# Other strips stream and other beats are set in the first layer, and TensorE adds more rows in the second

## What is computed

```python
def peer_ffn(h, w_q, sub_keys, u, v):          # per block of 128 tokens
    q = (xb @ w_q).reshape(BLK, PEER_HEADS, PEER_QDIM)               # 8 heads x 128
    s1 = einsum('thd,hkd->thk', q[..., :64], sub_keys[:, 0])         # 128 keys each
    s2 = einsum('thd,hkd->thk', q[..., 64:], sub_keys[:, 1])
    v1, i1 = top_k(s1, 16); v2, i2 = top_k(s2, 16)
    sc, ci = top_k(v1[..., :, None] + v2[..., None, :], 16)          # of 256 sums
    e = take(i1, ci // 16) * 128 + take(i2, ci % 16)                 # 16 experts per head
    g = softmax(sc)
    a = gelu(einsum('thkd,td->thk', u[e], xb)) * g
    return einsum('thk,thkd->td', a, v[e])
```

## Time and profile before

| | us |
|---|---|
| median of 3 runs | 2897.95 (2896.8 to 2899.27) |
| the profiled execution, its own time | 2902.58 |
| its span, first to last instruction | 2900.4 |

### The profile page before, as it was taken

The page is one execution under the profiler, slowest core; times in us unless marked ns, Lnnn a source line. Parts: engine busy times, 40 slices in busy tenths (PEclk is TensorE's granted clock), DMA queues, the critical chain, the costliest instruction groups (busy, mean ns, idle before and its releaser), DMA issues.

```text
span 2900.4 us, 27200 instructions
## 1 busy us (share of the span) xinstructions
PE 2284.9 (79%) x7394; PEld 1213.3 (42%) x7394; DVE 2184.6 (75%) x5166; ACT 1183.7 (41%) x3457; POOL 1244.1 (43%) x1049
## 2 busy tenths in 40 slices
PE   9779787788877887786887878877788878886567
PEld 8536442454424554243443434443354434432122
DVE  2688678876878757796688876988679876887664
ACT  3154334344343443445344453435534453433333
POOL 0254335443444333444434543354434444345655
PEclk9899999899999898998899988989889998988989
DMA  6599999999999999999999999999999999999998
GB/s 271 209 418 421 398 398 416 421 421 403 415 420 421 420 375 420 420 418 421 421 393 406 422 421 420 389 416 421 421 402 406 421 421 421 399 421 421 422 422 350
DMA packets 170817, 1170.27 MB, mean 403 GB/s; under 512 B 19668, under 2 KB 19928, under 8 KB 36136
## 3 DMA queue, kind: packets, MB, share of 16 engines
q0 software_dynamic: 147456, 1073.81, 89.7%
q1 hardware_dynamic: 23208, 94.74, 8.3%
HBM read 1164.28 MB, written 4.19 MB: 403 GB/s over the span
## 4 chain that ended last, share of the span: by engine, by line
DMA 28%; DVE 14%; PE 11%; issue 6%; POOL 3%; ACT 3%; POOLq 0%; DVEq 0%; ACTq 0%
DMA ring<-in_uv,pick 26%; PE acc L1723 6%; DVE ring L1094 4%; POOL ring L666 3%; PE ps L1514 3%; DVE side L1085 1%; DMA xc<-h 1%; DMA stream<-in_strips 1%; ACT diag L1368 1%; DVE arena L969 1%; DVE arena L950 1%; DVE arena L1040 1%; DVE arena L1044 1%; DVE arena L951 1%; DVE arena L1031 1%
## 5 line engine op out<-in xcount | busy, mean ns | idle before, releaser
L666 POOL DMA_INDIRECT ring<-in_uv,pick x1024 | 1239.7, 1211 | 1630.5 <-PE acc L1723 1092.9
L1723 PE MATMUL acc<-ring,diag 128*128 128x512 f32 x2988 | 1542.5, 659 | 465.3 <-ACT diag L1368 462.3
L1094 DVE CUSTOM_DVE_ANT_0 ring<-ring,h_now 128x1024 f32<-128x1024 f32 x1024 | 1235.4, 1222 | 490.2 <-DMA ring<-in_uv,pick 474.0
L1723 PEld LDWEIGHTS acc<-ring,diag 128*128 128x128 f32 x2988 | 582.6, 207 | 1287.7 <-ACT diag L1368 702.8
L1357 ACT ACTIVATE gelu<-dots 128x1 f32<-128x1 f32 x1024 | 206.1, 201 | 1264.6 <-DVE dots L1094 1258.0
L1085 DVE SCALAR_TENSOR_TENSOR side<-ring,coef,side 128x1024 f32<-128x1024 f32 x270 | 346.0, 1281 | 23.1 <-ACT coef L1360 23.0
L1360 ACT ACTIVATE coef<-gate,gelu 128x1 f32<-128x1 f32 x1024 | 302.0, 295 | 33.2
L1368 ACT ACTIVATE diag<-ident,coef 128x128 f32<-128x128 f32 x747 | 300.1, 402 | 29.8 <-PE acc L1723 5.5
L1514 PE MATMUL ps<-resident,actT 128*128 128x256 f32 x896 | 220.3, 403 | 14.5 <-ACT actT L1169 14.5
L1514 PEld LDWEIGHTS ps<-resident,actT 128*128 128x128 f32 x896 | 178.1, 202 | 58.9 <-issue 18.2
L1481 PE MATMUL ps<-actT,stream 128*128 128x128 f32 x960 | 124.9, 291 | 23.6 <-DMA stream<-in_strips 22.7
(11 more groups left out here) (198 smaller groups left out, 1454.6 us busy)
## 6 DMA issues: line engine op xcount, KB each, us to landing
stream<-in_strips SPq DMA_DIRECT2D x102, 512.0 KB
resident<-in_strips SPq DMA_DIRECT2D x18, 1024.0 KB, 12.9
ring<-in_uv,pick POOLq DMA_INDIRECT x1024
ring<-in_strips SPq DMA_DIRECT2D x9, 1024.0 KB, 19.6
arena<-in_keys SPq DMA_DIRECT2D x8, 512.0 KB
xc<-in_x SPq DMA_DIRECT2D x4, 512.0 KB
h<-arena SPq DMA_DIRECT2D x4, 512.0 KB, 11.4
xc<-h SPq DMA_DIRECT2D x4, 512.0 KB
```

Of the source, the lines that this page charges most:

```text
L666: pool.indirect_dma_start(ring[:, n % SLOTS, :], None, tables[layer], bass.IndirectOffsetOnAxis(ap=pick[:, col:col + 1], axis=0),).then_in ...
L1094: dve.tensor_tensor_reduce(ring[:, slot, 0:D], ring[:, slot, 0:D], h_now[:], 1.0, 0.0, ALU.mult, ALU.add, dots[:, slot:slot + 1]).then_inc ...
L1723: m = pe.matmul(acc[:, b * 512:(b + 1) * 512], diag[:, turn % 4, :], ring[:, slot, D + b * 512:D + (b + 1) * 512], start=(r == 0 and i == ...
```

## The change

In the first layer the resident strips are 5, 7, 9, 11, 13 and 15 to 18 (v1, v3, r1, r3, out1, out3, pq0 to pq2); 0 to 4, 6, 8, 10, 12, 14 and 19 pass. The beats of stages 1 and 2 are set anew, mostly earlier and further apart; those of stage 0 and of the second layer stay. `VECTOR` changes for "gla" (34 rows per stage instead of 37, none or one in rounds 0 to 2) and for "swa" (none from round 7 on: 19 instead of 34). SP loads the opening's strips in order of number, the keys of the first layer after all its passing strips, the first five resident strips of the second layer after "r" and "y" instead of "v", and in the second layer the bias, the other four resident strips, gain and keys after the first passing strip. POOL's wait for pq1 goes.

```diff
-STREAMED = tuple(s - RESIDENT for s in STRIPS)
+KEPT = ((5, 7, 9, 11, 13, 15, 16, 17, 18), (0, 1, 2, 3, 4, 5, 6, 7, 8))
+PASSING = tuple(tuple(n for n in range(STRIPS[layer]) if n not in KEPT[layer]) for layer in range(2))
+STREAMED = tuple(len(p) for p in PASSING)
...
-SAYS = ({11: "r", 15: "y", 16: "pq0", 17: "pq1", 18: "pq2", 19: "pq3"},
-        {8: "y", 9: "pq0", 10: "pq1", 11: "pq2", 12: "pq3"})
-DONE = [[SAYS[layer].get(n) for n in range(RESIDENT, STRIPS[layer])] for layer in range(2)]
+SAYS = ({1: "q", 3: "k", 19: "pq3"}, {9: "pq0", 10: "pq1", 11: "pq2", 12: "pq3"})
+DONE = [[SAYS[layer].get(n) for n in PASSING[layer]] for layer in range(2)]
...
-GAIN_AT = (13 - RESIDENT, 10 - RESIDENT)
+GAIN_AT = (PASSING[0].index(14), PASSING[1].index(10))
...
     "gla": (
-        ((1, 4, 7),) * 3 + ((0, 2, 4, 6),) + ((1, 4, 7),) * 2 + ((0, 2, 4, 6),) + ((1, 3, 5, 7),) +
-        ((0, 3, 6),) + ((2, 6),) + ((1, 4),) + ((2, 6),) + ((4,),) + ((),) * 3),
+        ((1,),) + ((),) + ((4,),) + ((0, 2, 4, 6),) + ((1, 3, 5, 7),) * 2 + ((0, 2, 4, 6),) + ((1, 3, 5, 7),) +
+        ((0, 2, 4, 6),) + ((1, 3, 5, 7),) + ((1, 4, 7),) + ((4,),) + ((),) * 4),
     "swa": (
-        ((1, 4, 7),) * 2 + ((0, 2, 4, 6),) + ((0, 4),) + ((1, 5),) + ((0, 3, 6),) + ((2, 6),) +
-        ((1, 4, 7),) * 2 + ((2, 6),) + ((1, 3, 5, 7),) + ((0, 3, 6),) + ((),) * 4),
+        ((1, 4, 7),) * 2 + ((0, 2, 4, 6),) + ((0, 4),) + ((1, 5),) + ((0, 3, 6),) + ((2, 6),) + ((),) * 9),
...
     "gla": {
-        "pe": {"hT": 7, "q0": 12, "q1": 24, "k0": 29, "k1": 38, "v0": 43, "v1": 45, "v2": 49, "v3": 52, "attn": 56,
-               "r0": 56, "r1": 56, "r2": 60, "upd": 62, "r3": 62, "o0": 64, "o1": 64, "oT": 69, "out0": 71,
-               "out1": 73, "out2": 76, "out3": 79, "h2T": 84, "pq0": 84, "sc0": 86, "pq1": 88, "sc1": 90, "pq2": 94,
-               "sc2": 94, "pq3": 105, "sc3": 118},
...
+        "pe": {"hT": 7, "q0": 11, "q1": 15, "k0": 18, "k1": 22, "v0": 26, "v1": 28, "v2": 31, "v3": 33, "attn": 38,
+               "r0": 40, "r1": 43, "r2": 46, "upd": 49, "r3": 50, "o0": 54, "o1": 55, "oT": 61, "out0": 64,
+               "out1": 68, "out2": 72, "out3": 76, "h2T": 82, "pq0": 83, "sc0": 86, "pq1": 88, "sc1": 91, "pq2": 94,
+               "sc2": 97, "pq3": 104, "sc3": 112},
...
             def load_kept_ahead(prep):
 
-                said_by(sp, "pe", before(prep), "v")
+                said_by(sp, "pe", before(prep), "r")
                 for n in range(AHEAD):
 
+                    if n == 4:
+                        said_by(sp, "pe", before(prep), "y")
                     released(sp, pick_number(BLOCKS - 2, AHEAD_AT + n - 1, 0))
...
                 for n in range(STREAMED[prep.layer]):
-                    if n == GAIN_AT[prep.layer]:
+                    if n == GAIN_AT[prep.layer] + opening:
+
+                        if prep.layer == 1:
+                            if prep.first:
+                                load_kept_rest(prep)
+
+                            said_by(sp, "pe", prep, "o3")
+                            sp.dma_start(bias_out, b_out).then_inc(bias_loaded, 16)
 
                         said_by(sp, "pe", prep, "oT")
...
+                if prep.layer == 0:
+                    load_keys(prep)
...
-                    elif SAYS[0].get(RESIDENT + n, "r") not in ("r", "y", "pq0"):
-
-                        said_by(pool, "pe", Prep("gla", 0), SAYS[0][RESIDENT + n])
-                        alone(pool, passed["pool"])
...
             def left(prep, n, bank, side):
...
                 for c in range(2):
                     for k in range(KT):
+                        if c == 0 and k % CUT == 0:
+                            cut_loaded(prep, n, k // CUT)
                         i = pe.matmul(ps[:, bank, (2 * side + c) * P:(2 * side + c + 1) * P],
                                       w[:, k, c * P:(c + 1) * P], actT[:, k, :], start=(k == 0),
                                       stop=(k == KT - 1))
+                        if c == 1 and k % CUT == CUT - 1:
+                            cut_done(prep, n, k // CUT, i)
                 return i
```

More of the change, by code:

```diff
@@ L416, in in_ring, with passing @@
         def in_ring(prep, n):
-            return prep.first and prep.layer == 0 and RESIDENT <= n < RESIDENT + SLOTS
+            return prep.first and prep.layer == 0 and n in PASSING[0][:SLOTS]
+        def passing(prep, n):
+            return n in PASSING[prep.layer]
         def weight(prep, n):
-            if n < RESIDENT:
-                return resident[:, n]
+            if not passing(prep, n):
+                return resident[:, KEPT[prep.layer].index(n)]
             if in_ring(prep, n):
-                return ring[:, n - RESIDENT, :].rearrange("p (k c) -> p k c", k=KT)
+                return ring[:, PASSING[0].index(n), :].rearrange("p (k c) -> p k c", k=KT)
             return stream
@@ L511, in load_kept @@
             def load_kept(prep, n):
-                sp.dma_start(resident[:, n].rearrange("p k c -> p (k c)"), strips[prep.layer][n])\
+                sp.dma_start(resident[:, n].rearrange("p k c -> p (k c)"),
+                             strips[prep.layer][KEPT[prep.layer][n]])\
                   .then_inc(res_loaded[n], 16)
             def load_kept_ahead(prep):
-                said_by(sp, "pe", before(prep), "v")
+                said_by(sp, "pe", before(prep), "r")
                 for n in range(AHEAD):
+                    if n == 4:
+                        said_by(sp, "pe", before(prep), "y")
                     released(sp, pick_number(BLOCKS - 2, AHEAD_AT + n - 1, 0))
@@ L528, in load_kept_rest, with load_keys @@
                     load_kept(prep, n)
+            def load_keys(prep):
+                said_by(sp, "pe", prep, "y")
+                sp.dma_start(keysT, (keys0, keys1)[prep.layer]).then_inc(keys_loaded, 16)
             def load_streamed(prep):
-                if prep.layer == 1:
-                    said_by(sp, "pe", prep, "o3")
-                    sp.dma_start(bias_out, b_out).then_inc(bias_loaded, 16)
                 opening = prep.first and prep.layer == 0
-                if opening:
-                    for n in range(SLOTS):
-                        sp.dma_start(ring[:, n, :], strips[0][RESIDENT + n]).then_inc(ring_loaded[n], 16)
                 for n in range(STREAMED[prep.layer]):
-                    if n == GAIN_AT[prep.layer]:
+                    if n == GAIN_AT[prep.layer] + opening:
[4 more added lines that the diff above has]
+                            sp.dma_start(bias_out, b_out).then_inc(bias_loaded, 16)
                         said_by(sp, "pe", prep, "oT")
@@ L546, in load_streamed @@
                         sp.dma_start(ffn_gain, gain_ffn[prep.layer:prep.layer + 1, :]).then_inc(gain_loaded, 16)
-                    if n == KEYS_AT[prep.layer]:
-                        said_by(sp, "pe", prep, "y")
-                        sp.dma_start(keysT, (keys0, keys1)[prep.layer]).then_inc(keys_loaded, 16)
+                        if prep.layer == 1:
+                            load_keys(prep)
                     for c in range(CUTS):
@@ L559, in load_streamed @@
                         sp.dma_start(stream[:, c * CUT:(c + 1) * CUT, :].rearrange("p k c -> p (k c)"),
-                                     strips[prep.layer][RESIDENT + n, :, c * CUT * STRIP:(c + 1) * CUT * STRIP])\
+                                     strips[prep.layer][PASSING[prep.layer][n], :, c * CUT * STRIP:(c + 1) * CUT * STRIP])\
                           .then_inc(slot_loaded[c], 16)
+                if prep.layer == 0:
+                    load_keys(prep)
             def preps(prep, after):
-                if prep.first:
-                    load_kept_rest(prep)
                 load_streamed(prep)
@@ L578, in _, with load_opening @@
                 sp.dma_start(dst, src).then_inc(consts_loaded, 16)
-            for n in range(RESIDENT):
-                load_kept(Prep("gla", 0), n)
+            def load_opening(begin, end):
+                for n in range(begin, end):
+                    if n in KEPT[0]:
+                        load_kept(Prep("gla", 0), KEPT[0].index(n))
+                    elif n in PASSING[0][:SLOTS]:
+                        i = PASSING[0].index(n)
+                        sp.dma_start(ring[:, i, :], strips[0][n]).then_inc(ring_loaded[i], 16)
+            load_opening(0, 9)
             for dst, src in ((ggla[:], gla_gain),
@@ L584, in _ @@
                 sp.dma_start(dst, src).then_inc(consts_late, 16)
+            load_opening(9, STRIPS[0])
             load_streamed(Prep("gla", 0))
@@ L1437, in strip @@
             def strip(prep, n):
-                if n < RESIDENT and prep.first:
-                    pe.wait_ge(res_loaded[n], 16 * (prep.layer + 1))
+                if not passing(prep, n) and prep.first:
+                    pe.wait_ge(res_loaded[KEPT[prep.layer].index(n)], 16 * (prep.layer + 1))
                 return weight(prep, n)
@@ L1445, in cut_loaded, with cut_done @@
```

(17 more changed lines are left out.)

4 lines of the change are left out of this document (1 added, 3 removed), and 19 rows, old and new, of the table AT.

## The result

The changed kernel takes 2904.09 us (median of 22 runs), the kernel before 2898.74 us (22 runs beside them). The medians lie 5.4 us apart; the ratio taken over the runs, which is used from here on, is smaller: 1.0012, 95% interval [1.0006, 1.0017]. It is 3.5 us slower (1.7 to 4.9), inside the bound of 0.2%, where I had forecast 2891, that is, faster. Single runs far from all others (5130.15 us here, 10727.64 and 5848.65 us in two experiments) are left out of the ratios. The two profiled executions differ the other way (spans of 2896.0 and 2900.4 us): of the changed kernel the fastest of its runs was profiled, of the one before a run above its median.

What follows compares the result with a forecast made beforehand. Transfers, with a ceiling of 422 GB/s, were taken to bound the kernel. The profiled 2902.58 us less 11 (first layer) plus 4 (second layer) gave 2895.6, and the runs' median 4.6 lower gave 2891 us; range 2875 to 2907.

Steps and rivals of the forecast that it cites:

- First layer, 11 us won: Stages 0 to 2: 12.2 us won from less lateness behind streamed strips, less 1 for TensorE without slack; bounds 3 to 18.
- Sum 53 us of lateness, and 20.8 us were lost with it: 0.39 us per us: Stages 0 to 2 before: streamed strips 17, 18 and 18 us late, set against 20.8 us lost in transfer dips.
- The early run, 8.6 us lost: Streamed strips q0, q1, k0, k1, v0: 10 us late in stage 0, 6 each in stages 1 and 2, at 0.39.
- Second layer, 4 us lost: Stages 3 to 6, rows of rounds 7 to 15 moved to TensorE: 4 x 2.5 x 0.39; bounds 4 won, 10 lost.
- The sum there is 80 - 8 + 15 x 1.75 = 98 of 100 us: Second layer, stage 5: TensorE's busy time with a faster clock and 15 more rows, just full.
- pq strips 2.5 us later in four stages: Second layer: some TensorE waits can't be filled, so pq strips come 2.5 us later, at 0.39 us lost per us.
- (a): Early run takes back all if loads among gathers take longer; break-even spacing 14.8 us; 2898 to 2902; chance 0.15 with (d).
- my own sign of being wrong: Forecast is wrong if q and k strips stand 15 us apart or more, stages 3 to 6 lengthen over 4 us each, or opening moves.
- (b): TensorE becomes the bound in rounds 7 to 15 of the second layer, 20 us lost, 2907; chance 0.18.
- (c): Both layers win: strip spacing 6 us or less, no run late, 20.8 plus 4 us won, 2873; chance 0.17.
- (d): Nothing changes because the dips are VectorE's, in the choice of experts; chance 0.15 together with (a).
- Opening and queues, 0: Opening's strip order, pq3 and POOL's wait, and what SP's queue loads when: no time won or lost.

Runs made afterwards that it cites:

- stage 0 spread out: Changed kernel with the old "swa" rows, and stage 0's q0 to v1 moved to beats 37, 42, 47, 52, 57, 58; ratio 0.9993 to the kernel before.
- the first layer alone: The changed kernel with the old rows of "swa" for VectorE; ratio 1.0025 to the kernel before, 7 us lost.

## Why the prediction was wrong

**First layer, 11 us won: wrong.** The step that failed is "Sum 53 us of lateness, and 20.8 us were lost with it: 0.39 us per us", and with it the term 20.8. It put every late dip down to the strips and took all of them as won ("at 0.39 that loses 8.6 us, so 12.2 are won"). In the same stretches the changed kernel still loses 7.8 + 1.2 + 0.4 = 9.4 us: stages 1 and 2 gave back 10.7 of their 12.3 us, stage 0 gave back 0.7 of its 8.5. In stage 0 stalls behind strips had covered waits for others. ScalarE's mask (beat 73) and VectorE's state0 (77) are written at later beats than the pieces of TensorE that need them (upd at 70, o0 at 74), which costs nothing while a strip holds TensorE behind the picks. Without that stall TensorE waited for them: 7.6 us, then (every other strip, the mask moved) 6.0 in the next place. The dip stayed until state0 and silu were moved too. In the changed kernel itself, behind the early run, moving them was not enough, so what keeps its late dip is open. I had named the wait that would go (it went, 17.7 to 2.9 us) and not asked what would be late next on the engine that is freed. A smaller slip: the 53 left out r1 to r3 of stage 0 (beats 66 to 72), 5 us late by the same reckoning, which would make the rate 0.36.

**The early run, 8.6 us lost: the mechanism was right, the size too small.** The lateness came out at 39.6 us less 26 = 13.5 in stage 0 and 49 less 42 = 7 in stages 1 and 2, sum 27.5 against my 22. Its price is about 9 us (stage 0 spread out) and 5 us (stages 1 and 2 with the old beats), 14 in all, or 0.5 us per us; each of the two is good to some 4 us, so that the rate differs from 0.39 (10.7 us) is not shown. The trace of the first layer alone gives the sum without these differences: in its early stretches it loses 5.1 + 5.7 + 4.1 = 14.9 us, in the late ones (379, 420 and 420 GB/s) 11.0 instead of 20.8. That is 14.9 less 9.8, 5 us lost, where 7 (4.6 to 9.9) were measured.

**Second layer, 4 us lost: wrong in sign.** "The sum there is 80 - 8 + 15 x 1.75 = 98 of 100 us" was right (97 us, clock 0.99). The step that failed is "pq strips 2.5 us later in four stages", each at 0.39. The strip pq1 of stages 3 to 6 starts 269.6, 259.5, 258.7 and 261.3 us into its stage before, and 269.2, 259.2, 260.1 and 258.0 in the changed kernel: later in stage 5 alone, by 1.4 us. On the average over the kernels with the old and with the new rows, stages 4 to 6 are shorter by 0.9 to 1.0 us each. The Trainium skill, page "TensorE: Matmul & The Clock Gate", section "Part 1: The HAM clock gate", has activity release the throttled state: the trace agrees (0.90 to 0.99), and the 4 us that my sum gave by that rule alone were nearer than mine. Whether the gain is the clock's or comes from VectorE, which has 90 us less to do there (1304 to 1215), was not told apart.

**The rivals.** (a) was right in kind: the early run took back what was won, and more. Its break-even was not: the twelve early spacings have a mean of 12.6 us, far below 14.8, because less was to be won than I put into it. Nor is the spacing one number: where the transfers run at 419 to 420 GB/s it is 15.1 to 15.7 us (stage 0 spread out), and 15.4 between the strips at 230.97 and 246.39 above (15 or more was my own sign of being wrong), while the 11.3 of the prediction was read inside a dip (in the kernel before, 356 GB/s from 1000 to 1025 us and 391 from 1025 to 1050). That loads take longer beside running gathers, the condition of (a), fits these rows; no run was made for it. (b) fell: TensorE is the fullest engine there, and the five stages of the second layer are 3 us shorter. (c) fell: spacings of 10.2 to 15.4 us, none near 6; the rule of turns between queues, in the Trainium skill, page "DMA: Bandwidth & Descriptors", section "Queues, rings and completion order", does not give this trace. (d) may hold for the end of stage 0 in the changed kernel.

**Opening and queues, 0: right.** Stage 0 starts at 107.1 us against 107.2.

**What stays open.** One profile of a first-layer stage is good to some 3 us only: stages 1 and 2 take 355.3 and 371.9 us before, 358.0 and 375.5 in the kernel that differs from it in the second layer alone. Shares of single stages below that size are not shown here. Open too are the late dip of stage 0 in the changed kernel and what is left of the dips of stages 1 and 2 with every other strip streamed.

## What to carry to other kernels

A stall on one engine can hide waits that are written for a late engine: before counting a stall as won, read what that engine needs next and at which beat it is written. With one buffer for streamed weights, space the loads by the measured spacing, in every stage by that stage's own beats; strips that alternate between kept and streamed did this here with the old schedule of stages 1 and 2 as well as with the new. Read a rate such as "lost time per us of lateness" from a run that removes the lateness, not from two sums that stand side by side.

## What was not expected of the hardware

A load on SP's queue takes long while gathers are in flight. The changed kernel, DMA issues of stage 2 and of stage 3 (KB each, median us from issue to landing), where the gathers run and the loads go out singly:

```profile
resident<-in_strips SPq DMA_DIRECT2D x5, 1024.0 KB, 9.6
...
resident<-in_strips SPq DMA_DIRECT2D x4, 1024.0 KB, 9.1
```

A megabyte at 422 GB/s would be 2.5 us; it takes 9.1 to 9.6. The nine such loads of the opening, issued one behind another with no gather in flight, have a median of 19.9 us, so issue to landing also holds the time in line. The half megabytes of a reloaded strip lie in spacings of 10.2 to 15.4 us.

And TensorE, given 81 more rows, did them in 111 us more busy time, 1.37 us for a row of four matmuls, less than the 1.75 of a row at full clock. The mean over all matmuls of this kind fell from 659 to 643 ns; whether the added rows are cheap or the rows that it had already ran faster is not told by these sums.
